# FFN input products by seven products of halves, with the FFN output multiplied out one inner tile at a time

## The reference, cut to what matters

```
x = x + mixer(rmsnorm(x))
g, u = split(rmsnorm(x) @ w_in, 2)      # w_in 1024 x 5632
x = x + (silu(g) * u) @ w_out           # w_out 2816 x 1024
```

## Time and profile before

| | us |
|---|---|
| median of 3 runs (2798.23 to 2802.04) | 2801.71 |
| the profiled execution | 2803.01 |
| its span, first to last instruction | 2801.2 |
| PE busy, share of the span | 96% |
| DVE, ACT, POOL busy | 37%, 32%, 39% |
| mean granted clock of PE | 0.984 |

### The profile page before, as it was taken

One profiled execution on the slowest core, in us unless ns is written; L12 is line 12 of the kernel. 1 busy time (PEld: TensorE's weight loads), 2 busy tenths in 40 slices (PEclk: granted clock), 3 DMA queues, 4 the chain that ended last, 5 costly groups with the idle time before them and its releaser, 6 DMA issues.

```text
span 2801.2 us, 44064 instructions
## 1 busy us (share of the span) xinstructions
PE 2676.4 (96%) x17524; PEld 2474.0 (88%) x17524; DVE 1044.1 (37%) x1221; ACT 891.2 (32%) x1557; POOL 1104.1 (39%) x488
## 2 busy tenths in 40 slices
PE   6898999999779999999999999999999999999997
PEld 4666666666579999999999999999999999999997
DVE  4665666666542321221221333443232122122223
ACT  4366655666732321111111231111232111111123
POOL 2765666765224332332332452222433233233334
PEclk9999999999899999999999999999999999999999
DMA  8666777777551111111111121111111111211112
GB/s 275 213 228 237 238 273 265 243 248 239 175 202 45 45 43 55 45 41 49 42 48 53 32 59 46 45 45 46 45 45 38 53 45 38 60 42 41 53 34 80
DMA packets 279581, 290.64 MB, mean 104 GB/s; under 512 B 12915, under 2 KB 238292, under 8 KB 279334
## 3 DMA queue, kind: packets, MB, share of 16 engines
q1 hardware_dynamic: 256898, 271.17, 30.3%
q10 hardware_dynamic: 22420, 16.82, 1.9%
q0 software_dynamic: 144, 1.05, 0.1%
HBM read 267.76 MB, written 21.28 MB: 103 GB/s over the span
## 4 chain that ended last, share of the span: by engine, by line
PE 81%; DMA 5%; POOL 5%; DVE 3%; ACT 3%; issue 2%; SPq 1%; ACTq 0%; DVEq 0%; POOLq 0%
PE PS L1298 70%; POOL kpage L698 3%; PE PS L1517 2%; DMA kpage<-in_cache_k 2%; PE PS L1519 2%; PE PS L1518 2%; PE PS L1456 1%; DMA vpage<-in_cache_v 1%; PE PS L1420 1%; ACT probs L942 1%; PE PS L1479 1%; POOL w_lo L688 1%; DMA out<-raw 1%; DVE nmax L1899 1%; DVE s_raw L1855 1%
## 5 line engine op out<-in xcount | busy, mean ns | idle before, releaser
L671 POOL TENSOR_TENSOR w_lo<-raw,w_hi 128x1024 fp32r<-128x1024 f32 x192 | 463.2, 2412 | 1204.0 <-ACT w_hi L849 1204.0
L849 ACT ACTIVATE w_hi<-raw 128x1024 fp32r<-128x1024 f32 x192 | 203.8, 1061 | 1253.7 <-PE PS L1298 1242.8
L1298 PE MATMUL PS<-a_hi,w_hi 128*128 128x344 f32 x2688 | 570.5, 321 | 1.1 <-ACT rinv L880 1.1
L1298 PE MATMUL PS<-a_lo,w_hi 128*128 128x344 f32 x2688 | 570.3, 320 | 0.0
L1298 PE MATMUL PS<-a_hi,w_lo 128*128 128x344 f32 x2688 | 567.5, 319 | 0.0
L1761 DVE SCALAR_TENSOR_TENSOR t<-PS,rinv 128x1032 f32<-128x1032 f32 x112 | 138.1, 1233 | 876.0 <-PE PS L1298 874.5
L1298 PEld LDWEIGHTS PS<-a_lo,w_hi 128*128 128x128 f32 x2688 | 455.0, 189 | 0.0
L1298 PEld LDWEIGHTS PS<-a_hi,w_hi 128*128 128x128 f32 x2688 | 452.2, 188 | 1.3 <-ACT rinv L880 1.3
L1298 PEld LDWEIGHTS PS<-a_hi,w_lo 128*128 128x128 f32 x2688 | 447.8, 188 | 0.0
L698 POOL TENSOR_TENSOR kpage<-kpage,q_bc 128x1024 f32<-128x1024 f32 x128 | 304.9, 2397 | 126.2 <-DMA kpage<-in_cache_k 95.6
L1298 PE MATMUL PS<-b_hi,w_hi 128*128 128x344 f32 x1440 | 307.8, 322 | 11.0 <-DVE b_lo L2130 10.9
(11 more groups left out here) (249 smaller groups left out, 2894.8 us busy)
## 6 DMA issues: line engine op xcount, KB each, us to landing
kpage<-in_cache_k SPq DMA_DIRECT2D x128, 512.0 KB, 4.5
vpage<-in_cache_v SPq DMA_DIRECT2D x128, 512.0 KB, 5.1
raw<-in_w_ffn_in SPq DMA_DIRECT2D x88, 512.0 KB, 3.8
raw<-in_attn_w_qkvf SPq DMA_DIRECT2D x24, 512.0 KB, 5.0
vpage<-in_attn_w_qkvf SPq DMA_DIRECT2D x24, 512.0 KB, 5.3
raw<-in_w_ffn_out SPq DMA_DIRECT2D x32, 384.0 KB, 3.4
raw<-in_conv_w_in SPq DMA_DIRECT2D x24, 512.0 KB, 3.8
raw<-in_w_ffn_out SPq DMA_DIRECT2D x32, 320.0 KB, 3.1
```

The costliest lines, as they stand in the source:

```text
L671: gp.tensor_tensor(w_lo[s][:, 0:kts, 0:cols], raw[s][:, 0:kts, 0:cols], w_hi[s][:, 0:kts, 0:cols].bitcast(F32), ALU.subtract).then_inc(w_l ...
L849: act.activation(w_hi[s][:, :, 0:cols], raw[s][:, :, 0:cols], ACT.Copy).then_inc(w_hid[s], 1)
L1298: ins = pe.matmul(g[:, b, :], w[:, k, :], x[:, k, b * TB:(b + 1) * TB], start=k == 0 and n == 0, stop=k == kts - 1 and n == 2)
```

## The change

In the FFN, the gate and up products of an inner tile are four quadrant products of halves in each of two groups. Columns are halved (`HN` = 516) and input features are halved (`HK` = 4 tiles); the gate and up weights are the two rows of a 2 x 2 block matrix. The eight half products are replaced by seven products of sums of weights and sums of activations, each 4 tiles x 3 x 2 blocks of 258 columns = 24 matmuls (168 for an inner tile). They go to four pairs of banks (`pairbank`), and DVE combines them (seven additions of 516 columns, `iv` counts them).

- **Weights.** `w_lows`, `w_highs`: POOL makes four sums of 128 x 512 and seven low parts of 128 x 512 for each inner tile, ACT seven high copies. Each combination has one buffer.
- **Activations.** `sums_pass` takes the place of the norm's work in the `w_o` and `w_cout` passes: ACT writes `x_res` times the norm's weight in two halves and squares it, DVE forms the sums (`half_sums`), ACT their high parts, DVE their low parts (`low_sums`), in all 7 x 4 tiles of 516 columns. For this the two passes are cut in two, over input tiles 0 to 3 and 4 to 7, with an addition to `x_res` after each.
- **Output product.** With the sums in memory there is room for two inner tiles only. So `out_tile` multiplies each inner tile out by itself: 8 output tiles of 9 matmuls, with 8 additions to `x_res` (`add_out`), after the next inner tile's seven products. The last two inner tiles are multiplied out together (`last_first`, `last_product`).
- **Order at the FFN's end.** In layer 0 the next weights' `high` and `low` stand behind all eight tiles' norm work. `rinv` is no longer applied at read-out, but by two multiplications of 1032 columns in SBUF.
- Loops of the FFN are written out.

```diff
...
+    HN, HK = T // 2, KT // 2
+    COMBO = [1, 0, 3, 2, 5, 6, 4]
+    PAIRBANK = [0, 1, 2, 3, 0, 2, 3]
+    FIRST, STEADY = [0, 1, 2, 3, 4, 5, 6], [0, 1, 3, 4, 2, 5, 6]
+    FIRST_SUMS, STEADY_SUMS = [1, 2, 5, 3], [1, 2, 3, 5]
+    MSEQ = [0, 4, 1, 5, 2, 6, 3, 7]
...
-            def out_loads(w, row, kts, first_pair=0):
-
-                with counted_loop(sp, first_pair, KT // 2, {wl[0]: 1, wl[1]: 1}) as i:
-                    load_w(0, w_tile(w, row, kts, i * (2 * P)), kts)
-                    load_w(1, w_tile(w, row, kts, i * (2 * P) + P), kts)
+            def out_loads(w, row, seq, first=0):
+                for i in range(first, KT):
+                    load_w(i % 2, w_tile(w, row, 4, seq[i] * P), 4)
...
+                for j in range(1, HID):
+                    if j == 1:
+                        sp.wait_ge(wls, 7 * jj + 5)
+                    else:
+                        sp.wait_ge(w_lod[0], lows[0] + j - 1)
+                    gate(j)
+                    sp.wait_ge(wls, 7 * (jj + j))
+                    upper(j)
+                    sp.wait_ge(wss, 4 * (jj + j + 1))
+                    outer(j - 1, 0)
+                sp.wait_ge(wls, 7 * (jj + HID))
+                outer(HID - 1, 1)
+                wl[0].value, wl[1].value = lows[0] + HID - 2, lows[1]
...
+                low_(0)
+                sum_(1)
+                sum_(2)
+                low_(1)
+                if j == 0:
+                    yield
+                    sum_(5)
+                    low_(2)
+                    sum_(3)
+                    low_(3)
+                    low_(4)
+                else:
+                    sum_(3)
+                    low_(3)
+                    low_(4)
+                    sum_(5)
+                    low_(2)
+                low_(5)
+                low_(6)
...
+            def ffn_lows(l, last_square):
+                w = w_lows(l, 0)
+                next(w)
+                last_square()
+                for _ in w:
+                    pass
+                for j in range(HID):
+                    if j > 0:
                         low(0)
-                        low(1)
-                        gp.wait_ge(bhi, hi_c.up())
-                        gp.tensor_tensor(b_lo[:, bass.ds(j, 1), :].rearrange("p a t -> p (a t)"), t1[:, :],
-                                         b_hi[:, bass.ds(j, 1), :].rearrange("p a t -> p (a t)").bitcast(F32),
-                                         ALU.subtract).then_inc(blo, 1)
-                    end = c == len(CHUNKS) - 1
-                    out_lows(last=last and end, final=end)
+                        inner_low(j - 1)
+                    if j < HID - 1:
+                        for _ in w_lows(l, j + 1):
+                            pass
+                inner_low(HID - 1)
+                low(1)
+                gp.wait_ge(mms, 7 * HID * (l + 1))
+                empty_sum(s2)
...
+            def halves(i, norm):
+                m, s = MSEQ[i], i % 2
+                act.wait_ge(ev[s], evc[s].up())
+                at = 1 if m < HK else 5
+                act.activation(c_f32[:, at:at + 2, m % HK, :], x_res[:, m, :].rearrange("p (h n) -> p h n", h=2), ACT.Copy,
+                               scale=vecs[:, m, NORMS[norm]:NORMS[norm] + 1]).then_inc(ahi, 1)
+                squares_free()
+                squares(x_res[:, m, :], f1)
+            ctc = Count(ctd)
+            def high_sums(i):
+                m = MSEQ[i]
+                act.wait_ge(ctd, ctc.up())
+                c = slice(0, 2) if m < HK else slice(2, 7)
+                act.activation(c_hi[:, c, m % HK, :], c_f32[:, c, m % HK, :], ACT.Copy).then_inc(chi, 1)
+            def sums_pass(l, norm):
+                high(0, 4)
+                high(1, 4)
+                for i in range(KT - 1):
+                    if i + 2 < KT:
+                        high(i % 2, 4)
+                    halves(i, norm)
+                    if i > 0:
+                        high_sums(i - 1)
+                w = w_highs(l, 0)
+                next(w)
+                halves(KT - 1, norm)
+                high_sums(KT - 2)
+                next(w)
+                high_sums(KT - 1)
+                next(w)
+                roots()
+                for _ in w:
+                    pass
...
+            def ffn_highs(l, norm):
+                for j in range(HID):
+                    jj = HID * l + j
+                    if j > 0:
+                        act.wait_ge(w_raw[0], wr[0].value + 16 * (2 * (j - 1) + 3))
+                        for s in range(2):
+                            act.wait_ge(mm[s], done[s].value + 1 + 4 * (j - 1))
+                        act.activation(w_hi[0][:, :, :], raw[0][:, :, :], ACT.Copy).then_inc(w_hid[0], 1)
+                        inner_high(j - 1)
+                    act.wait_ge(mms, 7 * jj + 1)
+                    act.activation(two(f0[:, 0:HN]), pairbank(0), ACT.Copy).then_inc(iu, 1)
+                    if j < HID - 1:
+                        for c in w_highs(l, j + 1):
+                            if c == 5:
+                                gate_silu(jj)
+                    else:
+                        gate_silu(jj)
+                act.wait_ge(w_raw[1], wr[1].value + 16 * (HID + 1))
+                act.wait_ge(mms, 7 * HID * (l + 1))
+                act.activation(w_hi[1][:, :, :], raw[1][:, :, :], ACT.Copy).then_inc(w_hid[1], 1)
+                inner_high(HID - 1)
...
+                    for m in range(KT):
+                        s = m % 2
+                        squares_free()
+                        act.wait_ge(ev[s], evc[s].up())
+                        normed(m, x_res[:, m, :], norm, s3)
+                    high(0)
+                    high(1)
...
+                for c in range(7):
+                    pe.wait_ge(wls, 7 * jj + at[c])
+                    if c == 0:
+                        pe.wait_ge(iv, 8 * jj)
+                        for s in range(2):
+                            pe.wait_ge(ev[s], evd[s].value + 1)
+                    if c == 2 and j == 0:
+                        next_norm(f0)
+                        pe.wait_ge(rq, rqc.up())
+                        pe.wait_ge(rq, rqc.up())
+                    if c == 4:
+                        pe.wait_ge(iu, jj + 1)
+                    if c == 5:
+                        pe.wait_ge(iv, 8 * jj + 1)
+                    if c == 6:
+                        pe.wait_ge(iv, 8 * jj + 4)
+                    out = pairbank(PAIRBANK[c])
+                    x = COMBO[c]
+                    for k in range(HK):
+                        if j == 0:
+                            pe.wait_ge(alo, lo_parts.value + 2 * k + (1 if x < 2 else 2))
+                        for n, (w, h) in enumerate(((W_hi[c], c_hi), (W_hi[c], c_lo), (W_lo[c], c_hi))):
+                            for b in range(2):
+                                ins = pe.matmul(out[:, b, :], w[:, k, :], h[:, x, k, b * (HN // 2):(b + 1) * (HN // 2)],
+                                                start=k == 0 and n == 0, stop=k == HK - 1 and n == 2)
+                    ins.then_inc(mms, 1)
...
+            def out_tile(l, j):
+                pe.wait_ge(iv, 8 * (HID * l + j + 1) + 6)
+                pe.wait_ge(w_lod[0], wlo[0].up())
+                pe.wait_ge(blo, bl.up())
+                for m in range(KT):
+                    pe.wait_ge(ev[m % 2], evd[m % 2].up())
+                    inner_steps(m, [((j % 2, 0), True, True)]).then_inc(mm[m % 2], 1)
...
+            def last_first():
+                pe.wait_ge(w_lod[0], wlo[0].up())
+                pe.wait_ge(blo, bl.up())
+                for m in range(2):
+                    pe.wait_ge(ev[m], evd[m].up())
+                    inner_steps(m, [(K20, True, False)])
+                pe.wait_ge(w_lod[1], wlo[1].up())
+                pe.wait_ge(blo, bl.up())
+                for m in range(2):
+                    inner_steps(m, [(K21, False, True)]).then_inc(mm[m], 1)
+            def last_product(m):
+                pe.wait_ge(ev[m % 2], evd[m % 2].up())
+                inner_steps(m, [(K20, True, False), (K21, False, True)]).then_inc(mm[m % 2], 1)
...
+            def ffn(l):
+                in_pair(l, 0)
+                for j in range(1, HID):
+                    in_pair(l, j)
+                    if j < HID - 1:
+                        out_tile(l, j - 1)
...
+            def half_sums(i):
+                m = MSEQ[i]
+                k = m % HK
+                dve.wait_ge(ahi, ah.up())
+                def part(c):
+                    return c_f32[:, c, k, :]
+                before = ctc.value
+                ctc.up()
+                if m < HK:
+                    dve.tensor_tensor(part(3), part(1), part(2), ALU.subtract)
+                    dve.tensor_tensor(part(0), part(2), part(1), ALU.subtract).then_inc(ctd, 1)
+                else:
+                    dve.wait_ge(ctd, before)
```

(53 more changed lines are left out.)

453 lines of the change are left out of this document (265 added, 188 removed).

## The result

The changed kernel takes **2997.34 us** (median of 4 runs, 2991.33 to 3002.35) against 2801.88 us (2798.23 to 2802.76) of the kernel before, taken on the same chip: ratio **1.0696**, 95% interval 1.0678 to 1.0714. It is slower, as forecast, but by 195.5 us where the forecast said 57, and it lies above the range. The profiled execution has a span of 2995.6 us.

A forecast was written before the change was run, and what follows sets the result against it. PE's own matmul stream was taken to bound the FFN. Terms -113.5 + 84.8 + 2 + 11 + 38 + 27 + 8 = +57.3 us gave a 2859 us median; range 2806 to 2915, the main forecast's own 2825 to 2893.

The forecast's parts named there:

- seven products in 44 inner tiles: FFN: 168 matmuls of 258 columns replace 144 of 344, 2.58 us less per inner tile, -113.5 us.
- 40 times `out_tile`: FFN output per inner tile: PE waits for DVE's additions, 2.12 us each time, +84.8 us.
- `w_o`'s start: Start of `w_o`: halved products no longer cover the wait for residual and weights, +11 us.
- `sums_pass` and FFN start, twice: Passes before each FFN: DVE and POOL exclude each other, PE idles, 19 us each with the clock, +38 us.
- end of layer 0: FFN's end: the next weights stand behind all eight tiles' norm work, 25 us idle plus 2 for clock, +27.
- The edges: Costs outside the steady FFN: `w_o` +11, the two passes +38, end of layer 0 +27, end of layer 1 +8.
- the fourth rival: FFN's third and sixth products wait for POOL's late weights; each further us costs 40 us, 2899 with one; 10%.
- the cover of 9 us: FFN: POOL finishes the next weights at about 24 us of a period, PE wants them at 33.6.
- the steady part: FFN's repeating inner tile: PE sets a period of 33.6 us, with POOL, DVE and ACT hidden at no cost.
- Cheaper narrow products: FFN's 258-column matmuls take 0.108 us each, saving 86 us more: 2773, faster; 8%.
- The steady clock: FFN: PE restarts at half clock after each period's 1.6 us wait, 72 us more: 2931; 10%.
- Overlapping edges: Passes, layer 0's end and output tiles: DVE and POOL collide little, 53 us less: 2806, down to 2788; 10%.

The follow-up runs named there:

- experiment 1: Changed kernel with ACT again making the convolution's weights two products ahead, `w_cout`'s first two included: 2893.11 us, ratio 1.0326.
- experiment 2: Kernel before, with only the convolution's order changed so ACT's weights stand behind DVE's result: 2918.51 us against 2799.35, ratio 1.0424.
- Experiment 6: Changed kernel with the residual loaded in eight tiles and `w_o`'s third and fourth weight loads behind the first two: 2986.03 us, ratio 1.0662.
- Experiment 7: Changed kernel with ACT's wait for POOL's square sum moved behind the normed copy in layer 0's last eight output tiles: 2989.32 us, ratio 1.0676.
- experiment 3: Changed kernel where the next first product waits for one bank group's additions only, the second product for the other's: 2939.55 us, ratio 1.0498.
- the last experiment: Changed kernel with all edits that paid, plus reordered work before `w_cout` and at each layer's end: 2788.97 us against 2799.46, ratio 0.996.

## Why the prediction was wrong, step by step

The terms of the sum against what the traces show (the passes' and the ends' with the half clock after their waits):

| term | forecast, us | measured, us |
|---|---|---|
| seven products in 44 inner tiles | -113.5 | -105.6 (20.29 us for one, not 20.11) |
| 40 times `out_tile` | +84.8 | +85.2 (13.48 us, less 11.35 of work) |
| second inner tile | +2 | +1.8 |
| `w_o`'s start | +11 | +11.1 (23.5 less `w_cout`'s 12.4) |
| `sums_pass` and FFN start, twice | +38 | about +44 |
| end of layer 0 | +27 | about +32 |
| end of layer 1 | +8 | about +9 |
| convolution and the wait before `w_cout` | none | **+113.8** |

The measured column adds to 191, but counts one restart of 2.3 us twice, that behind the wait of 14.7 us (end of layer 0, and convolution); without it, it is 189. The attention was 3.2 us shorter in this execution, so the terms have 197.7 us to explain, and some 9 of them are not assigned.

Two small slips of the working: 72 matmuls in 11.37 us are 0.1579 us each, not the 0.1576 that the sum uses, which is worth some 2 us; and 16 to 21 us less 7.75 of work are 8.25 to 13.25 idle, not 8.5 to 13.5.

**The step that failed: "The edges".** The list goes from `w_o` over `sums_pass` to the end of each layer and stops at "the convolution's first product". What lies behind it was costed at nothing without a sentence that said so, although the change rewrites ACT's loop there; the description of the change and its excerpt of the diff leave that loop out too. The forecast asked of each stage how the seven products change it; it did not ask of each rewritten loop whether it still issues the same things in the same order. That alone is 113.8 of the 138 us by which the forecast fell short; experiment 1 takes 107.3 of them away by the order alone, and experiment 2 puts such a loss into the kernel before. It was no rival either: the fourth rival has POOL's weights late, but in the FFN, and there the cover of 9 us held (no wait of PE for them in the steady part).

**Right: what bounds, and the steady part.** Starts of PE in the changed kernel: four of `out_tile`'s output tiles, the first product behind them, and the same product one inner tile later.

```profile
1410.21 1.12 PE L1943 MATMUL PS<-wb,w_hi 128*128 128x344 f32 x6
...
1413.12 1.21 PE L1943 MATMUL PS<-wb,w_hi 128*128 128x344 f32 x6
...
1416.14 1.22 PE L1943 MATMUL PS<-wb,w_hi 128*128 128x344 f32 x6
...
1419.16 1.21 PE L1943 MATMUL PS<-wb,w_hi 128*128 128x344 f32 x6
...
1423.69 0.48 PE L1931 MATMUL PS<-a_all,wb 128*128 128x258 f32 x2 [1.42 <-DVE x_res L2449]
...
1457.46 0.48 PE L1931 MATMUL PS<-a_all,wb 128*128 128x258 f32 x2 [1.42 <-DVE x_res L2449]
```

The period is 33.77 us (forecast 33.6, before 34.0), one output cycle 3.02 us (forecast 3.01), the whole of `out_tile` 13.48 us (forecast 13.46). The 258-column matmul takes 0.1204 us (166 of them from 1424.02 to 1444.01; forecast 0.1197, from the 256-column row). Over 168 matmuls that is 0.12 us of the 0.18 by which a tile's products are longer than forecast; the rest is PE's first pair after the wait (0.33 us instead of 0.24). DVE's multiplication by `rinv` met POOL and took 2.05 us at 1408.32, and was hidden, as the working said.

**Right: `w_o`.** PE went on 23.9 us after `w_o`'s start (forecast 24.0), after a wait of 9.67 us (forecast 12) and at half clock. Experiment 6 shows the residual ahead of the weights in the queue as a reason: with most of it behind them, 4.17 us of the wait are left.

**Nearly right in size: `sums_pass`.** PE waited 3.2 us within the pass of `w_o`, then 6.26, 6.97 and 1.41: 17.8 us, and 19.2 in the second layer, against 17 forecast without the clock. The lag was smaller than the 6 us assumed (2.0 us of wait at the last tile); the start's chain was longer. The clock was under-sized: two waits, each with a slow restart, cost 3.5 to 4 us in a pass, not 2.

**Mis-sized: the end of layer 0.** The chain was put at 3.95 us for an output tile, 47.9 us in all; it measured 4.83 and 54.4 (1646.82 to 1701.22). The sum took DVE and ACT in turn, but in the code ACT's next copy stands behind its wait for POOL's sum of the squares (2.60 us), which is a longer loop: ACT copy, ACT square, POOL. Experiment 7 takes the wait off the loop and gets 3.73, below the forecast's figure.

**The rivals.** Cheaper narrow products: refuted by the interval. The steady clock: refuted, the FFN's window from 960 stands at 0.99 and stretches between its waits at 1.00; a wait of 1.42 us every 33.8 did not lower the clock. Overlapping edges: refuted in the main, since most edges came out at or above their price. The forecast's sign was right, and its own mechanism, without the convolution, gives 80.7 us: 2882, inside both of its ranges. That is 23 us above the sum all the same, because most terms came out a little dearer than priced.

**Where the gain of seven products in place of eight is.** It is real, 105.6 us. In the changed kernel the output tiles, which were moved to make room for it, gave 85.2 back, and the edges some 96. With one wait placed better (experiment 3) 57 of the 85 return, so the loss was not inherent in doing the output one inner tile at a time. The kernel before has hardly a wait to win (PE waits 22 us in all from 780 us to its end), while the last experiment still has some 30 at the FFN's starts. Some of the orders mended on the way (the residual's transfer, `w_cout`'s first weights) might shorten the kernel before by a few us too; no run tried that.

## What to carry to other kernels

Read a diff engine by engine, loop by loop, also where it looks like a rewrite of the same thing: for each loop write down which product's weights an engine prepares in place n, and what it waits for just before. A lead of two that becomes zero is invisible in the busy shares (ACT was at 33%) and cost about as much as the arithmetic saved (104 to 107 us in experiment 1, against 105.6). When a wait covers several buffers, ask which of them the next instruction really writes; and when an output is split so that each addition stands alone, the last addition is the one that counts. Before two engines that share operands' memory are made to start together, check whether the one that gets later is the one on the path.

## What the runs showed of the hardware

- **The clock after a wait.** Six matmuls of 344 columns that take 1.11 us in a stream took 2.06 to 2.09 us after every wait of 5.11 us or more, 1.84 after one of 4.17 and 1.20 after one of 2.76; two waits of 4.03 us were followed by 1.53 in one kernel and by 2.09 in another. After the waits of 1.42 us in every period there was nothing to see (clock 1.00). The length of the last wait does not tell it alone: the third short wait of `w_o`'s pass was followed by a slow group, the same wait in `w_cout`'s pass was not.

```profile
899.91 1.75 PE L1514 MATMUL PS<-wb,w_hi 128*128 128x344 f32 x6 [2.02 <-POOL w_lo L754]
...
2188.31 1.22 PE L1514 MATMUL PS<-wb,w_hi 128*128 128x344 f32 x6 [2.02 <-POOL w_lo L754]
```

  The granted clock was 0.57 from 899.9 to 903.0 us and 1.00 from 2188.3 to 2192.0. In the eight kernels that have both waits (2.0 to 2.1 us), the first group took 1.53 to 2.04 us in `w_o`'s pass in seven and 1.22 in one, and 1.20 to 1.22 in `w_cout`'s pass in all eight. Why is open. The changed kernel's granted clock in the 3.5 us after one of the convolution's restarts, and in 4.1 us of 258-column matmuls at the FFN's start:

```profile
1752.60:1756.10 3.50, 3.48 (x12) 3.48 (x13) 0.00 (x0) 0.00 (x0) 2.30 (x1) 0.50 0.54 150
...
913.60:917.70 4.10, 4.07 (x18) 3.88 (x18) 4.10 (x2) 1.46 (x3) 4.02 (x2) 0.54 0.00 0
```

  0.50 is the lower level, 1.2 GHz. The convolution has eight such restarts in its 18.4 us of added PE time, 2.3 us each: a wait of 12.5 us costs almost 15. The Trainium skill (TensorE: Matmul & The Clock Gate, What's actually happening) knows only two levels. The rows agree: windows at 0.50 and at 1.00 occur, and the values between them can be mixtures of both.
- **Which operations of DVE POOL holds up.** DVE's addition from PSUM is untouched: it takes 1.22 us while POOL works on, while half sums with two SBUF operands take 1.76 or 2.92 us instead of 0.68. The changed kernel's DVE, then POOL:

```profile
898.64 3.91 DVE L2478 TENSOR_TENSOR c_lo<-c_f,a_all 128x2580 fp32r<-128x2580 f32 x1
...
902.48 1.22 DVE L2449 TENSOR_TENSOR x_res<-PS,x_res 128x1032 f32<-128x1032 f32 x1
903.62 1.76 DVE L2470 TENSOR_TENSOR c_f<-c_f 128x516 f32<-128x516 f32 x1
...
900.22 4.61 POOL L764 TENSOR_TENSOR f<-f 128x1032 f32<-128x1032 f32 x1 [0.36 <-ACT f L1018]
```

  POOL's operation takes 4.61 us here and 2.38 where it starts first (906.01), so it is held up as well: it begins at 900.22 and ends 2.28 us after DVE's low parts do (902.55). DVE's half sum started at 903.62 in turn ends 0.55 us after POOL's operation does (904.83). The Trainium skill (SBUF — State Buffer, Who interferes with whom) says that the two lock each other out and that it depends on both inputs being in SBUF; these rows agree.
